# Routed experts: output rows stored by an indirect transfer that leaves out empty slots, and two weight loads that wait for the third expert's slot numbers

## The chip, the cores and the metric

The kernel runs on one core of a Trainium2 chip. The metric is the device time of the program in microseconds; lower is better. The engines are PE (TensorE, matrix products), DVE (VectorE), ACT (ScalarE), POOL (GpSimd) and SP (SyncE, which only issues transfers). Transfers run on 16 DMA engines that all queues share: q1 is SP's queue, q10 ACT's, q0 POOL's.

## The reference

A transformer layer in float32 on 512 tokens of width 1024: a mixer (attention and a state-space branch), cross-attention to 256 memory rows, a mixture of experts, and then a second layer of other form (gated and block-compressed attention and a feed-forward part). The change lies in the mixture of experts:

```python
scores = sigmoid(x2d @ w_router)                 # 512 tokens x 64 experts
# 4 of 8 groups, then 8 experts per token; weights normalised, times 2.5
top_idx = top_k(masked(scores + router_bias), 8)
...
# expert e: its tokens' rows x through two products
out_e = (silu(x @ w_gate[e]) * (x @ w_up[e])) @ w_down[e]   # 1024 -> 256 -> 1024
routed[token] += weight * out_e
y = routed + swiglu(x2d, w_sh_gu, w_sh_down)     # the shared expert
```

512 tokens in 8 experts each are 4096 pairs, 64 per expert on average.

## The kernel before, in words

**Slots.** Each expert has `CAP` = 96 slots. DVE counts, for each chosen expert of a token, the slot that it gets, and from it the row of a table in HBM: row 65 x slot + expert (`PITCH` = 65). An expert's slots fill from 0 up. POOL scatters the tokens' numbers into the table (`slot_table`) by indirect transfers, one round for each of the eight choices k: `scatter_ids(k)`, four transfers each. The table was filled with 512 (`T`) before, so an empty slot reads 512. Experts over 96 tokens have a path of their own, which isn't taken with these inputs. Round k writes the k-th choice of every token in the order of the experts' numbers, so column e of the table is complete after rounds 0 to e for e < 8, and after all eight for the rest.

**Slot numbers.** ACT loads column e of the table into SBUF (`index_column(e)`, after `ids_sent[e]`) for e < 8, and all others in one transfer (`idx_rest`). POOL gathers the rows of x of an expert by an indirect transfer (`gather(e)`) of 96 rows of 4 KB; a slot number over 511 is out of bounds, and no row is read for it.

**The loop over experts.** In `e_block(u, b)` (expert e = 4u + b), PE turns the rows of expert e + 1, multiplies those of e by its gate/up weights (2 MB), and puts in between the down products (1 MB of weights) of expert e - 2. ACT and DVE copy the three parts of an expert's output into `ye[e % 2]` (96 x 1024 f32), and ACT stores all 96 rows into the scratch `y` in HBM with `y_send`: a transfer of 96 rows of 4 KB, 260 KB apart. The copies into the same buffer for expert e + 2 wait until that store has landed (`y_stored`). In the end 32 indirect gathers fetch each token's 8 rows of `y` for the weighted sum.

**Weights.** SP issues them: four gate/up buffers and four down buffers. `refill(e, b)` asks for the gate/up weights of expert e + 4 when `gu_full` says that the product of expert e is done, then for down weights. The first ones are asked for in the order of their buffers' release. Two of them share ring buffers with the shared expert's last panels and are in the list `late`: the gate/up weights of expert 1 and the down weights of expert 0. They are issued when the first gather has landed; the gate/up weights of expert 3 follow them.

**Zeros.** The scratch `y` has a 65th column, which POOL zeroes with 96 rows (`y_pad`).

## Time and profile before

| what | value (us) |
| --- | --- |
| median of 3 runs | 2176.5 (2175.79 to 2177.84) |
| profiled execution, its own time | 2178.47 |
| its span, first to last instruction | 2176.6 |
| PE busy | 2013.4 (93% of the span) |
| DVE, ACT, POOL busy | 773.7, 472.2, 325.5 |
| mean granted PE clock, as a share of full speed | 0.976 |

The span is what the profile shows of the execution. All times of rows below are of this one execution and count from the start of its span. An instruction's row has its start, its duration, its engine and line, what it writes and reads, and in brackets the time its engine stood idle before and what ended that. Rows with q behind the engine's name are transfers being issued; their duration is the issue alone.

### The profile page before, as it was taken

The numbers are of one execution on the slowest core, as the hardware profiler recorded it, in microseconds if no ns is written. First come the engines' busy times: TensorE is split into PE (matmuls) and PEld (weight loads), VectorE is DVE, ScalarE is ACT, GpSimd is POOL, SyncE is SP. The second block draws the span as 40 slices with busy tenths as digits, with TensorE's granted clock in tenths as the row PEclk, the third lists the DMA queues.
The fourth block names the chain that finished last, engine by engine and source line by source line (L and its number), as shares of the span: only waits on it lengthen the run. The fifth ranks groups of instructions, "written<-read, shape, count | busy, mean of one in ns | idle before, by whom it ended". The sixth has DMA issues, their size and how long they took to land.

```text
span 2176.6 us, 25744 instructions
## 1 busy us (share of the span) xinstructions
PE 2013.4 (93%) x10002; PEld 932.7 (43%) x10002; DVE 773.7 (36%) x1606; ACT 472.2 (22%) x1043; POOL 325.5 (15%) x296
## 2 busy tenths in 40 slices
PE   7887999999997999998989999699989899999997
PEld 3334434445543344443334334345655444444443
DVE  5998781214265233332222335501374200000012
ACT  2234431110310333333333332210263000000000
POOL 0653260000025211101010104200032000000000
PEclk9898999999998999999999999899999999999999
DMA  5110014213245999999999977521310222222210
GB/s 227 48 39 1 10 58 163 77 49 126 97 151 180 352 397 400 402 395 390 383 386 384 397 274 254 217 87 68 117 40 1 77 77 77 77 77 77 69 39 29
DMA packets 68579, 368.43 MB, mean 169 GB/s; under 512 B 12194, under 2 KB 12450, under 8 KB 51616
## 3 DMA queue, kind: packets, MB, share of 16 engines
q1 hardware_dynamic: 45216, 300.95, 36.6%
q0 software_dynamic: 12960, 34.13, 4.4%
q10 hardware_dynamic: 10336, 32.45, 4.1%
q8 instruction: 43, 0.70, 0.1%
q14 instruction: 24, 0.20, 0.0%
HBM read 346.35 MB, written 29.92 MB: 173 GB/s over the span
## 4 chain that ended last, share of the span: by engine, by line
PE 69%; DMA 13%; DVE 9%; issue 5%; POOL 2%; ACT 1%; POOLq 0%; SPq 0%; ACTq 0%; DVEq 0%
PE bank L932 41%; PE bank L1263 12%; DMA slab<-w_exp_down 10%; PE bank L1473 6%; PE bank L941 2%; DVE slab L1894 1%; DVE slab L1897 1%; PE bank L1281 1%; DVE work L1891 1%; DVE s5x L1894 1%; POOL slot_table L2619 1%; DVE slab L1891 1%; PE bank L994 1%; DMA slab<-y_rows,yrow_i 1%; DMA slot_table<-tok_i,yrow_i 1%
## 5 line engine op out<-in xcount | busy, mean ns | idle before, releaser
L932 PE MATMUL bank<-slab,ring 128*128 128x512 f32 (+1 forms) x1488 | 632.7, 586 | 12.9 <-DMA ring<-stream 11.2
L932 PEld LDWEIGHTS bank<-slab,ring 128*128 128x128 f32 x1488 | 282.3, 191 | 358.2 <-issue 355.6
L932 PE MATMUL bank<-ring,slab 128*128 128x512 f32 (+1 forms) x608 | 252.6, 576 | 3.8 <-ACT slab L1506 2.0
L1263 PE MATMUL bank<-ring,slab 128*32 128x512 f32 x1536 | 231.7, 605 | 17.7 <-DMA slab<-w_exp_down 14.1
L1263 PE MATMUL bank<-slab 128*32 128x512 f32 x1536 | 227.2, 593 | 22.0 <-DMA ring<-w_exp_down 15.6
L1894 DVE TENSOR_TENSOR slab<-bank,slab 96x256 f32<-96x256 f32 (+3 forms) x120 | 63.8, 532 | 462.6 <-PE bank L932 296.5
L1271 PE MATMUL bank<-ring,slab 128*32 128x512 f32 x512 | 226.1, 594 | 0.0
L2338 DVE COPY slab<-bank 32x512 f32<-32x512 f32 x124 | 80.8, 688 | 407.9 <-PE bank L1271 407.9
L1271 PE MATMUL bank<-slab 128*32 128x512 f32 x480 | 215.0, 601 | 0.0
L932 PEld LDWEIGHTS bank<-ring,slab 128*128 128x128 f32 x608 | 115.6, 191 | 137.4 <-issue 129.4
L2554 POOL TENSOR_TENSOR small<-small 128x1 f32<-128x1 f32 (+2 forms) x30 | 23.0, 765 | 914.6 <-DVE small L1891 913.2
L1473 PE MATMUL bank<-ring,slab 128*128 128x512 f32 x352 | 151.3, 592 | 0.8 <-DVE slab L1894 0.8
L1263 PEld LDWEIGHTS bank<-ring,slab 128*32 128x32 f32 x1536 | 73.1, 111 | 150.7 <-issue 150.4
L2630 POOL DMA_INDIRECT slab<-x_rows,s5x x64 | 61.5, 960 | 507.4 <-PE bank L1225 477.5
L1263 PEld LDWEIGHTS bank<-slab 128*32 128x32 f32 x1536 | 70.5, 110 | 152.2 <-issue 144.3
L1473 PEld LDWEIGHTS bank<-ring,slab 128*128 128x128 f32 x352 | 66.8, 190 | 85.3 <-issue 83.7
L1732 ACT ACTIVATE slab<-bank 32x512 f32<-32x512 f32 x124 | 66.6, 584 | 105.9 <-PE bank L1271 97.4
L1688 ACT ACTIVATE slab<-bank 128x384 f32<-128x384 f32 x128 | 55.8, 488 | 143.5 <-DVE slab L2319 122.0
L1869 ACT ACTIVATE slab<-bank 128x512 f32<-128x512 f32 x22 | 13.1, 597 | 281.8 <-PE bank L932 281.8
L1225 PE MATMUL bank<-const_sb,slab 96*128 96x96 f32 x512 | 53.7, 249 | 13.1 <-DMA slab<-x_rows,s5x 12.2
L941 PE MATMUL bank<-const_sb,work 128*128 128x128 f32 x304 | 48.2, 293 | 18.1 <-DVE work L1891 14.1
L1506 ACT ACTIVATE slab<-bank 128x512 f32<-128x512 f32 (+2 forms) x40 | 22.7, 574 | 181.4 <-PE bank L932 171.6
(275 smaller groups left out, 2144.4 us busy)
## 6 DMA issues: line engine op xcount, KB each, us to landing
ring<-stream SPq DMA_DIRECT2D x171, 512.0 KB, 3.5
slab<-w_exp_gu SPq DMA_DIRECT2D x32, 2048.0 KB
ring<-w_exp_gu SPq DMA_DIRECT2D x32, 2048.0 KB
ring<-w_exp_down SPq DMA_DIRECT2D x32, 1024.0 KB
slab<-w_exp_down SPq DMA_DIRECT2D x32, 1024.0 KB
y_rows<-slab ACTq DMA_DIRECT2D x64, 384.0 KB
gb<-rows ACTq DMA_DIRECT2D x5, 512.0 KB, 5.3
slab<-x_fm SPq DMA_DIRECT2D x1, 2048.0 KB, 9.1
```

What stands on the lines that cost most here:

```text
L932: mm = nc.tensor.matmul(dst, lhs[k], rhs[k], start=(k == 0), stop=(k == len(lhs) - 1))
L941: mm = nc.tensor.transpose(tile(name, i)[0:parts, j * P:(j + 1) * P], x, ident)
L1225: mm = nc.tensor.transpose(bank[j][:, k * CAP:(k + 1) * CAP], xg[b][0:CAP, (4 * j + k) * P:(4 * j + k + 1) * P], ident[0:CAP, 0:CAP])
L1263: mm = nc.tensor.matmul(g_bank[32 * g:32 * g + 32, :], x[:, k, 32 * g:32 * g + 32], w[:, 512 * k:512 * k + 512], start=(k == 0), stop=(k = ...
L1271: mm = nc.tensor.matmul(bank[2 + 3 * t + half][96:128, :], h[:, c * CAP + 32 * t:c * CAP + 32 * t + 32], d[:, c * D + 512 * half:c * D + 5 ...
L1473: return nc.tensor.matmul(tile("fd", 4 * half + t)[:, :], actf[k][:, t * P:(t + 1) * P], panel("fd", 11 * half + k // 2)[:, (k % 2) * 512: ...
L1688: i = nc.scalar.activation(xe[b][:, 4 * j:4 * j + 4, :], bank[j][:, 0:4 * CAP].rearrange("p (k n) -> p k n", n=CAP), ACT.Copy)
L1732: i = nc.scalar.activation(ye[b % 2][0:32, 512 * half:512 * half + 512], bank[2 + half][96:128, :], ACT.Copy)
L1891: return nc.vector.tensor_scalar(out_, in_, s1, s2, op0, op1)
L1894: return nc.vector.tensor_tensor(out_, x, y, op)
L2338: i = nc.vector.tensor_copy(ye[b % 2][32:64, 512 * half:512 * half + 512], bank[5 + half][96:128, :])
L2630: pool.indirect_dma_start(xg[e % 2][0:CAP, :], None, scratch["x2"], bass.IndirectOffsetOnAxis(ap=slot_tok[:, e:e + 1].bitcast(U32), axis=0 ...
```

## The change

Stores: experts 0 to 3 and the last two, 62 and 63, are stored as before, by ACT. The 58 others are stored by POOL with an indirect transfer, `store_rows(e)`, behind the gather of expert e + 6. The list of target rows, `yrow_slot`, is made once by DVE in the block of the sixth expert from the slot numbers: 65 x slot + expert where the slot is filled, and beyond the scratch's bounds where it is empty, so that no row is written. Waits of ACT, DVE and POOL for the stores are split between `y_stored` (direct) and `y_sent` (indirect). The second four experts are written out ahead of the loops of ACT and DVE.

Zeros: since slots are left out, the whole first part of the scratch (96 x 65 = 6240 rows of 4 KB) is zeroed by one transfer that ACT issues before the first attention, in place of POOL's 96 rows.

Weights: the second item of `late` (down weights of expert 0), and with it what SP issues behind it, waits for `idx_landed[2]`, the slot numbers of the third expert.

```diff
@@ sync
-            for x in late:
+            for n, x in enumerate(late):
+                if n == 1:
+                    sp.wait_ge(idx_landed[2], 16)
                 panels_done(*x[:2])
                 x[2]()
@@ scalar
             s5_tables(8)
+            act.dma_start(scratch["y"][0:CAP * PITCH, :], a["zeros"].broadcast_to([CAP * PITCH, D])).then_inc(y_pad, 16)
             for h in range(H1 + 2):
...
-                    y_send(e - 3, (b + 1) % 2)
+                    if send:
+                        y_send(e - 3, (b + 1) % 2)
...
                     if steady:
-                        act.wait_ge(y_stored[b % 2], 16 * (2 * u + b // 2 - 1))
+                        if late:
+                            act.wait_ge(y_sent[b % 2], 16 * (2 * u + b // 2 - 3))
+                        else:
+                            act.wait_ge(y_stored[b % 2], 16 * (2 * u + b // 2 - 1))
...
-            with act.Fori(1, NE // 4 - 1) as u:
+            for b in range(4):
+                e_block(1, b, first=1, send=b < 3, late=False)
+            with act.Fori(2, NE // 4 - 1) as u:
@@ vector
+            for b in range(4):
+                e_block(1, b, first=1, late=False)
+                if b == 1:
+                    for k in range(TOPK):
+                        dve.wait_ge(idx_landed[k], 16)
+                    dve.wait_ge(idx_rest, 16)
+                    link(nc.vector.tensor_copy(slot_f, slot_tok))
+                    link(ts(slot_f, slot_f, T - 0.5, 65536.0, ALU.is_gt, ALU.mult))
+                    tt(yrow_slot, slot_f, row_id, ALU.add).then_inc(y_rows_ready, 1)
@@ gpsimd
-            pool.dma_start(y3[0:CAP, NE, :], a["zeros"].broadcast_to([CAP, D])).then_inc(y_pad, 16)
...
+            def store_rows(e):
+                if e == 4:
+                    pool.wait_ge(y_rows_ready, 1)
+                    pool.wait_ge(y_pad, 16)
+                pool.wait_ge(y0_act, e + 1)
+                pool.wait_ge(y1_dve, e + 1)
+                pool.wait_ge(y2_act, e + 1)
+                pool.wait_ge(y2_dve, e + 1)
+                pool.indirect_dma_start(scratch["y"][0:CAP * PITCH, :], bass.IndirectOffsetOnAxis(ap=yrow_slot[:, e:e + 1].bitcast(U32), axis=0),
+                                        ye[e % 2][0:CAP, :], None, bounds_check=CAP * PITCH - 1, oob_is_err=False).then_inc(y_sent[e % 2], 16)
...
                 gather(e)
+                if e >= 10:
+                    store_rows(e - 6)
+            for e in range(NE - 6, NE - 2):
+                store_rows(e)
```

On POOL, the program before has in the loop nothing but the gathers, one for each expert (the rows from the seventh expert's on; `slab` is the buffer of gathered rows, `x_rows` the rows of x in HBM, `s5x` the slot numbers):

```order
L2630 DMA slab<-x_rows,s5x 96x1024 [waits xtr_full,gathered0,idx_landed6]
L2630 DMA slab<-x_rows,s5x 96x1024 [waits xtr_full,gathered1,idx_landed7]
L2630 DMA slab<-x_rows,s5x 96x1024 [waits xtr_full,gathered0,idx_rest]
L2630 DMA slab<-x_rows,s5x 96x1024 [waits xtr_full,gathered1]
L2630 DMA slab<-x_rows,s5x 96x1024 [waits xtr_full,gathered0]
```

After the change the same place reads as follows (from the ninth expert's gather on; `y_rows` is the scratch y):

```order
L2657 DMA slab<-x_rows,s5x 96x1024 [waits xtr_full,gathered0,idx_rest]
L2657 DMA slab<-x_rows,s5x 96x1024 [waits xtr_full,gathered1]
L2657 DMA slab<-x_rows,s5x 96x1024 [waits xtr_full,gathered0]
L2669 DMA y_rows<-slab,s5x 6240x1024 [waits y1_dve,y2_act,y0_act,y2_dve,y_pad,y_rows_ready]
L2657 DMA slab<-x_rows,s5x 96x1024 [waits xtr_full,gathered1]
L2669 DMA y_rows<-slab,s5x 6240x1024 [waits y2_act,y2_dve,y1_dve,y0_act]
L2657 DMA slab<-x_rows,s5x 96x1024 [waits xtr_full,gathered0]
L2669 DMA y_rows<-slab,s5x 6240x1024 [waits y2_act,y2_dve,y1_dve,y0_act]
```

A store stands now between each two gathers, and a gather is issued only when the store ahead of it has its four waits behind it.

On SP, before, the loads at the end of the shared expert (`w_exp_gu` gate/up, `w_exp_down` down weights) are these:

```order
L817 DMA ring<-w_exp_gu 128x4096 [waits psum_full,gathered0]
L820 DMA ring<-w_exp_down 128x2048 [waits psum_full]
L817 DMA slab<-w_exp_gu 128x4096 [waits psum_full]
L817 DMA ring<-w_exp_gu 128x4096 [waits gu_full] x2
L817 DMA slab<-w_exp_gu 128x4096 [waits gu_full]
```

And after:

```order
L819 DMA ring<-w_exp_gu 128x4096 [waits psum_full,gathered0]
L822 DMA ring<-w_exp_down 128x2048 [waits psum_full,idx_landed2]
L819 DMA slab<-w_exp_gu 128x4096 [waits psum_full]
L819 DMA ring<-w_exp_gu 128x4096 [waits gu_full] x2
L819 DMA slab<-w_exp_gu 128x4096 [waits gu_full]
```

The order of the loads is the same; the second one has a new wait, and all loads behind it stand behind that wait too.

## Rows read from the trace of the kernel before

**Rows 1.** The page, section 1: busy us and share of the span.
```profile
PE 2013.4 (93%) x10002; PEld 932.7 (43%) x10002; DVE 773.7 (36%) x1606; ACT 472.2 (22%) x1043; POOL 325.5 (15%) x296
```

**Rows 2.** Windows of the loop: busy us by engine, granted clock, DMA share, GB/s.
```profile
790.00:965.00 175.00, 169.18 (x1714) 73.61 (x1710) 55.14 (x133) 58.32 (x133) 18.17 (x19) 1.00 1.01 399
965.00:1155.00 190.00, 169.37 (x1718) 71.08 (x1714) 55.12 (x133) 58.33 (x133) 18.18 (x19) 1.00 1.00 386
```

**Rows 3.** Waits of PE, 700 to 1300: total us, times, longest.
```profile
PE bank L1263 <- DMA ring<-w_exp_down: 15.6, 14, 1.8
PE bank L1263 <- DMA slab<-w_exp_down: 14.1, 14, 1.8
```

**Rows 4.** Timeline of SP: gate/up loads at experts 10, 29, 48.
```profile
791.86 0.33 SPq L817 DMA_DIRECT2D slab<-w_exp_gu  x1
967.03 0.33 SPq L817 DMA_DIRECT2D ring<-w_exp_gu  x1
1157.03 0.33 SPq L817 DMA_DIRECT2D ring<-w_exp_gu  x1
```

**Rows 5.** DMA queues in 965 to 1155: packets, MB, share of 16 engines.
```profile
q1 hardware_dynamic: 5527, 60.53, 82.0%
q10 hardware_dynamic: 2121, 7.44, 10.6%
q0 software_dynamic: 2118, 5.36, 7.5%
```

**Rows 6.** Queue q0 in 899.9:901, in 899.9:907, and in 983.5:984.6.
```profile
q0 software_dynamic: 22, 0.03, 8.8%
q0 software_dynamic: 112, 0.17, 6.5%
q0 software_dynamic: 20, 0.08, 19.1%
```

**Rows 7.** Timeline before the loop and in its start: us, duration, engine, [idle before].
```profile
672.11 0.33 SPq L817 DMA_DIRECT2D ring<-w_exp_gu  x1
673.82 0.72 SPq L817 DMA_DIRECT2D slab<-w_exp_gu  x1
674.68 0.99 POOL L2630 DMA_INDIRECT slab<-x_rows,s5x  x1 [0.30 <-issue]
683.98 1.54 PE L1225 MATMUL bank<-const_sb,slab 96*128 96x96 f32 x8 [8.85 <-DMA slab<-x_rows,s5x]
690.42 0.99 POOL L2630 DMA_INDIRECT slab<-x_rows,s5x  x1 [7.83 <-DMA s5x<-slot_table]
703.60 0.38 PE L1232 MATMUL bank<-const_sb,slab 96*128 96x96 f32 x2 [1.14 <-issue]
```

**Rows 8.** Window after the loop's start.
```profile
684.00:706.00 22.00, 19.92 (x126) 7.17 (x130) 6.33 (x14) 2.57 (x7) 10.04 (x11) 0.87 0.55 200
```

**Rows 9.** Timeline of POOL and ACT in the loop, and queue q0 in 909:915.2.
```profile
905.03 0.96 POOL L2630 DMA_INDIRECT slab<-x_rows,s5x  x1 [8.35 <-PE bank L1225]
...
905.77 0.32 ACTq L1712 DMA_DIRECT2D y_rows<-slab  x1
917.37 1.08 ACT L1732 ACTIVATE slab<-bank 32x512 f32<-32x512 f32 x2 [1.05 <-PE bank L1271]
920.72 0.38 ACT L1694 ACTIVATE slab<-bank 96x256 f32<-96x256 f32 x1 [2.28 <-PE bank L1263]
...
q0 software_dynamic: 110, 0.30, 12.7%
```

**Rows 10.** ACT at 157, that window, SP's first issues (min/median/max ns), q1 in 0:13.
```profile
157.43 1.28 ACT L1526 ACT_TABLE_LOAD   x1
...
157.00:225.00 68.00, 54.09 (x214) 29.52 (x212) 58.65 (x101) 30.33 (x74) 24.17 (x18) 0.87 0.01 2
...
L805 SPq DMA_DIRECT2D ring<-stream x12: 421/647/2285, 1.2 to 12.4; - x12
...
q1 hardware_dynamic: 589, 3.75, 77.3%
```

More of the change, by code:

```diff
@@ L650, in build @@
         ovn, ovincl, none64 = rt(64), rt(64), rt(64)
+        row_id, slot_f = rt(64)[0:CAP, :], rt(64)[0:CAP, :]
         wsum, wk = rt(4), sm(32)
@@ L658, in build @@
         slot_tok = s5x[0:CAP, 3072:3072 + NE].bitcast(I32)
+        yrow_slot = s5x[0:CAP, 3136:3200].bitcast(I32)
         no_token = s5x[0:120, 3072:3072 + NROW // 120].bitcast(I32)
@@ L750, in build @@
         gu_landed, dn_landed = [sem(f"gu_landed{j}") for j in range(4)], [sem(f"dn_landed{j}") for j in range(4)]
-        y_stored = [sem("y_stored0"), sem("y_stored1")]
+        y_stored, y_sent = [sem("y_stored0"), sem("y_stored1")], [sem("y_sent0"), sem("y_sent1")]
         xtr_full, xe_ready, gu_full, silu_ready = sem("xtr_full"), sem("xe_ready"), sem("gu_full"), sem("silu_ready")
@@ L759, in build @@
         diag_ready, pe_combined = sem("diag_ready"), sem("pe_combined")
-        combined, y_zeroed, y_pad = sem("combined"), sem("y_zeroed"), sem("y_pad")
+        combined, y_zeroed, y_pad, y_rows_ready = sem("combined"), sem("y_zeroed"), sem("y_pad"), sem("y_rows_ready")
         act_ready = sem("act_ready")
@@ L898, in _ @@
             for b in range(2):
-                sp.wait_ge(y_stored[b], 16 * NE // 2)
+                sp.wait_ge(y_stored[b], 48)
+                sp.wait_ge(y_sent[b], 16 * (NE // 2 - 3))
         @block.tensor
@@ L1707, in y_send @@
             def y_send(e, b):
+                if e == 0:
+                    act.wait_ge(y_pad, 16)
                 act.wait_ge(y2_act, e + 1)
@@ L1711, in y_send, with e_block @@
                 act.wait_ge(y2_dve, e + 1)
-                act.dma_start(y3[0:CAP, bass.ds(e, 1), :].rearrange("r e d -> r (e d)"), ye[b][0:CAP, :]).then_inc(y_stored[b], 16)
-            def e_block(u, b, first=0, last=NE):
+                act.dma_start(y3[0:CAP, e, :], ye[b][0:CAP, :]).then_inc(y_stored[b], 16)
+            def e_block(u, b, first=0, last=NE, send=False, late=True):
                 e = 4 * u + b
@@ L1750, in _ @@
             y_rest(NE - 3, 1)
-            y_send(NE - 3, 1)
             for b in range(2):
-                act.wait_ge(y_stored[b], 16 * (NE // 2 - 1))
+                act.wait_ge(y_sent[b], 16 * (NE // 2 - 3))
                 y_full(b, 5 - 5 * b, dnf_full, b + 1, yf_act)
@@ L1759, in _ @@
             for b in range(2):
-                act.wait_ge(y_stored[b], 16 * NE // 2)
+                act.wait_ge(y_stored[b], 48)
+                act.wait_ge(y_sent[b], 16 * (NE // 2 - 3))
             n_ov = act.value_load(ctrl_i[0:1, NOV:NOV + 1], min_val=0, max_val=NOV)
@@ L2319, in y_rest, with e_block @@
                 nc.vector.tensor_copy(ye[b][64:96, 768:1024], bank[4][96:128, 0:256]).then_inc(y2_dve, 1)
-            def e_block(u, b, first=0):
+            def e_block(u, b, first=0, late=True):
                 e = 4 * u + b
@@ L2335, in e_block @@
                     if steady:
-                        dve.wait_ge(y_stored[b % 2], 16 * (2 * u + b // 2 - 1))
+                        if late:
+                            dve.wait_ge(y_sent[b % 2], 16 * (2 * u + b // 2 - 3))
+                        else:
+                            dve.wait_ge(y_stored[b % 2], 16 * (2 * u + b // 2 - 1))
                     for half in range(2):
@@ L2342, in _ @@
                 e_block(0, b)
-            with dve.Fori(1, NE // 4) as u:
+            for b in range(4):
[7 more added lines that the diff above has]
+                    tt(yrow_slot, slot_f, row_id, ALU.add).then_inc(y_rows_ready, 1)
+            with dve.Fori(2, NE // 4) as u:
                 for b in range(4):
@@ L2350, in _ @@
             for b in range(2):
-                dve.wait_ge(y_stored[b], 16 * (NE // 2 - 1))
+                dve.wait_ge(y_sent[b], 16 * (NE // 2 - 3))
                 y_full(b, 5 - 5 * b, dnf_full, b + 1, yf_dve)
@@ L2355, in _ @@
             for b in range(2):
-                dve.wait_ge(y_stored[b], 16 * NE // 2)
+                dve.wait_ge(y_stored[b], 48)
+                dve.wait_ge(y_sent[b], 16 * (NE // 2 - 3))
             n_ov = dve.value_load(ctrl_i[0:1, NOV:NOV + 1], min_val=0, max_val=NOV)
@@ L2603, in _ @@
             nc.gpsimd.memset(none64, 0.0)
+            nc.gpsimd.iota(row_id, [[1, NE]], base=0, channel_multiplier=PITCH, allow_small_or_imprecise_dtypes=True)
             nc.gpsimd.memset(chosen[:, 256:320], 0.0)
@@ L2639, in _ @@
                 gather(e)
+                if e >= 10:
+                    store_rows(e - 6)
+            for e in range(NE - 6, NE - 2):
+                store_rows(e)
             pool.wait_ge(route_ctrl, 3)
             pool.wait_ge(xtr_full, NE)
-            pool.wait_ge(y_pad, 16)
             for b in range(2):
-                pool.wait_ge(y_stored[b], 16 * NE // 2)
+                pool.wait_ge(y_stored[b], 48)
+                pool.wait_ge(y_sent[b], 16 * (NE // 2 - 3))
             n_ov = pool.value_load(ctrl_i[0:1, NOV:NOV + 1], min_val=0, max_val=NOV)
```

2 lines of the change are left out of this document (1 added, 1 removed).

## The prediction

> **What bounds the kernel now.** The page first: TensorE (PE) is busy for 93% of the span [rows 1]. From 700 to 1300 us runs the loop over the 64 routed experts, and the windows show that the DMA engines are full there too, so I read it by stretches. From 790 to 965 us PE is busy for 169.2 of 175 us, from 965 to 1155 for 169.4 of 190, at the same granted clock of 1.00 and a DMA share of 1.01 and 1.00 [rows 2]. What ended PE's idle time in the loop was above all the down weights, 15.6 + 14.1 = 29.7 us [rows 3]. When it happened is read from SyncE (SP): it asks for a new gate/up matrix each time an expert's gate/up product is done, so its L817 rows are a clock of the experts. 19 experts from 791.86 to 967.03 take 9.22 us each; 19 from there to 1157.03 take 10.0 each [rows 4]. So the weights were ahead of PE at first, lost 0.8 us of their lead with each expert, and set the pace from about the 29th expert on. Less DMA work pays only there, or earlier by keeping the lead.
>
> **The bytes.** In 965 to 1155 the weights (q1) take 82.0% of the engines' time, the y stores (q10) 10.6%, the gathers (q0) 7.5% [rows 5]. The gathers carry 5.36 MB for 19 experts, 69 rows of 4 KB each out of 96; a y store always carries 96. The change makes 58 stores (experts 4 to 61) indirect and leaves empty slots out. 512 tokens in 8 experts each fill 4096 slots, 64 an expert, so it removes 58 x 32 = 1856 rows, 7.6 MB, and at the 386 GB/s of that stretch [rows 2] 19.7 us of DMA time. That would be the gain if every byte less brought the weights earlier.
>
> I doubt it, for a reason that the trace gives. A weight matrix is usable when all 16 engines have delivered their share, so the fullest engine counts, not the mean. How are the rows of an indirect transfer dealt out? A gather makes 112 packets: 96 rows, of which the empty ones are under 512 B, and 16 for the semaphore. The one read from 899.9 us moved 0.17 MB, 41 full rows; in its first 1.1 us it made 22 packets with 0.03 MB, about 7 full and 15 empty [rows 6]. Were the rows dealt in turn, each engine would have two or three full ones at its head, and 22 packets on 16 engines would nearly all be full. In a fuller expert's gather they are: 20 packets, 0.08 MB [rows 6]. So some engines have full rows only and others empty ones only: neighbouring slots, six by six, lie on one engine, and as an expert's slots fill from 0, the empty ones always fall to the last engines. The work per expert is then, for a full engine, 8.20 (weights, 0.820 x 10.0) + 1.06 (store) + 0.75 x 96/69 = 1.04 (gather) = 10.3 us, beside a measured period of 10.0 (packets overlap a little), and for the last engine 8.20 + 1.06 = 9.3. The change takes the empty store rows from the last engines only: 10.3 stays 10.3, and 9.3 becomes 8.2. By this the 7.6 MB are worth nothing, but that full engines share the memory with less traffic. The trace has no price for that; it lies between 0 and 0.34 us an expert (0.131 MB at 386 GB/s). I take 0.05, near the lower end, because it is a side effect of 3% of the traffic, over the 36 experts from the 29th on: 2 us.
>
> The Trainium skill ("DMA: Bandwidth & Descriptors", section "The descriptor swizzle") says that each engine of a transfer writes a fixed set of neighbouring partitions. By that rule, too, the empty rows lie on the same few engines, and the packets here agree; dealt evenly, the sum would be 19.7 us instead of 2.
>
> **The held weights.** After the shared experts PE stands still for 8.85 us, until at 683.98 the rows of the second expert have landed; their gather was issued at 674.68 [rows 7]. Just before, SP had issued 2 + 1 + 2 MB of weights, the first at 672.11 and the last at 673.82 [rows 7]. In the same load the third expert's slot numbers were on their way: GpSimd (POOL) waited 7.83 us for them, until 690.42 [rows 7]. The change lets only the 2 MB at 672.11 go; the down weights of the first expert and the gate/up weights of the fourth, behind them on SP, wait for the third slot numbers. 2.1 MB at 386 GB/s are 5.4 us, so the engines are free near 679 and the gather should land near 681 (gain 3), the slot numbers near 682. The held 3 MB run from there to 690, when the engines were used at 0.55 before (684 to 706 [rows 8]), and are first needed by the third and fourth experts, after 700. Behind the wait on SP stand the refills; the first needs the first expert's product, which starts after 684 anyway. The third gather comes some 7 us earlier, and the 1.14 us that PE waits at 703.6 [rows 7] can go. Bounds: 0 (the chain of ids and slot numbers waits elsewhere) and 5; I take 4. It counts although the weights set the end, since each refill follows PE's product and the engines are not yet full there [rows 8].
>
> **Added work, at nothing.** POOL issues a store behind each gather, another 0.96 us in a period in which it idles 8.35 [rows 9]. The store leaves at 906.3 instead of 905.77 and stands behind the gather on one queue; now the gather's last packets run until 915 [rows 9], so I put the store's end near 917. ACT's next copy into that buffer starts at 917.37, and 2.28 us are free behind it [rows 9]: a store up to 2 us later is hidden, and beyond that it delays each expert. DVE waits for the same stores, later in the period. Its three small operations on slot numbers stand in an engine busy for 55.1 of 190 us [rows 2]. The zeros, 6240 rows or 25.6 MB, are issued by ScalarE (ACT) at about 157.4, are 66 us of DMA work at 386 GB/s, and find engines that move 2 GB/s [rows 10]; nothing needs them before 700. Nothing, then, as long as ACT is free after its issue.
>
> Sum: 4 + 2 = 6 us. The profiled run took 2178.5 (span 2176.6) and the median is 2176.5; from the median the forecast is **2170.5 us**.
>
> **Rivals.**
> *The bytes count in full* (0.22). For it: the DMA share of 1.00 [rows 2]; with the last engines idle for 10% of the time it should be about 0.97. Then 19.7 us of DMA work go, PE has 29.7 us of such waits to give, and with the 4 at the start the time is 2153.
> *ACT is held by the zeros* (0.22; slower). At the start SP issued 16 transfers of 8 rows an engine in a row, and the issues grew to 2.29 us, from a least of 0.42 [rows 10]: with much in flight, an issue waits. Of those 144 packets an engine (8 rows and a semaphore each) 589/16 = 37 were through at 13 us [rows 10], so about 107 could be outstanding. The zeros are 390 an engine. If the limit is near 107, some 283 must drain first: 283/390 of 66 us = 48 us in which ACT computes no softmax, in a stretch in which it is busy for 30.3 of 68 us and PE waits on its chain [rows 10]. Price 48 less 6: 2218.5. It decides as soon as ACT is held for over 6 us. 
> *No net change* (0.20). The store lands 2 to 3 us late, ACT's copy slips and the experts from the 8th to the 61st pay 0.1 us each, 5 us, against the 6: 2175.5, within -4 to +4.
> *The forecast* (0.36), own range 2166 to 2174.
>
> **How the numbers follow.** 0.2%, 4.4 us, is about what a measurement of this kernel can tell from no change. Of the forecast's 0.36, 0.27 lie beyond it; with the 0.22 of the full bytes and 0.03 of no net change, faster is 0.52. Within it lie 0.09 + 0.13 = 0.22, slower are 0.22 + 0.04 = 0.26. The range must reach into both outer cases: 2151 below; above, the held case lies anywhere from some us to 48, and 2212 leaves about half of it out.
>
> **What would show it.** Right: the L817 rows again 10 us apart in the middle of the loop, PE waiting for down weights; PE's wait before the first expert near 6 us instead of 8.85; ACT's issue of the zeros under 1 us. Full bytes: periods of 9.2 to 9.5 throughout. Held: an issue of tens of us at 157, and PE behind ACT until 210. Late store: ACT waiting for y_rows in every period. The forecast is wrong above all if the issue holds ACT, or if a store's rows are dealt to the engines otherwise than a gather's.

## The result, and the profile after

The changed kernel took 2199.98 us (2198.62 to 2202.68, 4 runs), the kernel before 2177.1 on the same chip: a ratio of 1.0107 (95% interval 1.009 to 1.0125), 22.9 us slower. The forecast of 2170.5 has the wrong sign; the range held the value only because it reached out to a rival that did not happen.

The page of the profiled run after the change, against [rows 1] and [rows 3] (busy time and idle time before; then queues):

```profile
span 2196.8 us, 25741 instructions
PE 2020.9 (92%) x10002; PEld 933.0 (42%) x10002; DVE 773.8 (35%) x1609; ACT 472.9 (22%) x1043; POOL 382.4 (17%) x354
...
L1268 PE MATMUL bank<-ring,slab 128*32 128x512 f32 x1536 | 232.8, 607 | 30.2 <-DMA slab<-w_exp_down 27.0
L1268 PE MATMUL bank<-slab 128*32 128x512 f32 x1536 | 231.6, 601 | 30.4 <-DMA ring<-w_exp_down 22.2
```

PE waits 27.0 + 22.2 = 49.2 us for down weights, where it waited 29.7. The stretches of [rows 2], now:

```profile
790.00:965.00 175.00, 161.07 (x1631) 68.89 (x1624) 52.28 (x126) 56.23 (x128) 34.61 (x36) 1.00 0.99 366
965.00:1155.00 190.00, 163.39 (x1658) 68.81 (x1650) 54.41 (x132) 57.02 (x131) 34.61 (x36) 1.00 0.98 359
```

SyncE's gate/up issues are again the clock of the experts; these answer to [rows 4]:

```profile
791.97 0.33 SPq L819 DMA_DIRECT2D slab<-w_exp_gu  x1
...
865.73 0.33 SPq L819 DMA_DIRECT2D slab<-w_exp_gu  x1
875.28 0.33 SPq L819 DMA_DIRECT2D slab<-w_exp_gu  x1
885.68 0.33 SPq L819 DMA_DIRECT2D ring<-w_exp_gu  x1
...
1194.11 0.33 SPq L819 DMA_DIRECT2D slab<-w_exp_gu  x1
1206.38 0.33 SPq L819 DMA_DIRECT2D slab<-w_exp_gu  x1
...
1286.62 0.33 SPq L819 DMA_DIRECT2D slab<-w_exp_gu  x1
```

At 792 us the two kernels are level (791.86 before). The change costs nothing up to there, and everything behind it: the last of these issues is at 1286.62, before it was at 1265.78, 20.8 us of a span that is 20.2 longer. PE sets the pace only until 865.73, where it did until 967.03 [rows 4], eleven experts more; then 30 experts take (1194.11 - 885.68) / 30 = 10.28 us each, and the last nine, (1286.62 - 1194.11) / 9, as much; before, the last 30 take (1265.78 - 967.03) / 30 = 9.96. Fewer bytes are to be moved, and they move more slowly: 366 and 359 GB/s in place of the 386 of [rows 2] and more.

Where in an expert's period is the rate lost? The windows can be laid by the gather's issue on GpSimd. Its packets start some 4 us after it. For two gathers each, the 3 us that begin 1 us after the issue, and the 3 us that begin 5 us after it, before the change (issues at 1039.67 and 1049.74; the last column is GB/s, the one ahead of it the DMA engines' busy share):

```profile
1040.70:1043.70 3.00, 3.00 (x32) 1.10 (x28) 0.00 (x0) 0.89 (x3) 0.00 (x0) 1.00 1.04 423
1044.70:1047.70 3.00, 3.00 (x40) 1.26 (x32) 0.52 (x1) 0.44 (x2) 0.00 (x0) 1.00 1.03 388
1050.70:1053.70 3.00, 3.00 (x32) 0.92 (x28) 0.00 (x0) 1.17 (x3) 0.00 (x1) 1.00 0.99 404
1054.70:1057.70 3.00, 3.00 (x39) 1.14 (x31) 0.78 (x2) 0.39 (x2) 0.00 (x0) 1.00 1.02 391
```

And after it (issues at 1041.33 and 1051.83):

```profile
1042.30:1045.30 3.00, 3.00 (x32) 1.10 (x28) 0.00 (x0) 0.00 (x0) 0.95 (x2) 1.00 0.99 425
1046.30:1049.30 3.00, 3.00 (x36) 1.25 (x32) 0.00 (x0) 0.72 (x3) 0.00 (x0) 1.00 0.95 280
1052.80:1055.80 3.00, 3.00 (x32) 1.09 (x31) 0.00 (x0) 0.00 (x0) 0.95 (x2) 1.00 0.99 425
1056.80:1059.80 3.00, 3.00 (x36) 1.15 (x32) 0.00 (x0) 0.64 (x2) 0.00 (x0) 1.00 0.99 296
```

The engines are busy for 0.95 and 0.99 of the time there, but while the gather's rows move they carry 280 and 296 GB/s where they carried 388 and 391. The queues of the second stretch, before:

```profile
DMA packets 206, 1.16 MB, mean 388 GB/s; under 512 B 36, under 2 KB 36, under 8 KB 138
q1 hardware_dynamic: 73, 0.75, 65.1%
q10 hardware_dynamic: 64, 0.25, 22.8%
q0 software_dynamic: 69, 0.17, 15.0%
```

and after:

```profile
DMA packets 168, 0.84 MB, mean 280 GB/s; under 512 B 51, under 2 KB 51, under 8 KB 94
q1 hardware_dynamic: 82, 0.66, 74.8%
q0 software_dynamic: 86, 0.18, 20.6%
```

Before, 0.75 + 0.17 = 0.92 MB were read in 3 us, 307 GB/s, and 0.25 MB of y rows written beside them. After, 0.84 MB are moved in all, 280 GB/s, and no queue but the weights' and GpSimd's has a share in it: the store stands behind the gather in GpSimd's queue, and its rows go later, when reads alone would reach 425. The experiments ask what part of the change makes this.

### The profile page after: what moved, and what is told of

Its sections match the earlier page's. It is cut to its first block, busy times and chain, and to the rows that moved or that the text cites. A ratio compares the mean times of both kernels' runs of the same rounds, so it can differ in the third digit from the quotient of the medians.

```text
span 2196.8 us, 25741 instructions
## 1 busy us (share of the span) xinstructions
PE 2020.9 (92%) x10002; PEld 933.0 (42%) x10002; DVE 773.8 (35%) x1609; ACT 472.9 (22%) x1043; POOL 382.4 (17%) x354
## 4 chain that ended last, share of the span: by engine, by line
PE 67%; DMA 18%; DVE 9%; issue 4%; POOL 1%; ACT 1%; SPq 0%; POOLq 0%; DVEq 0%; ACTq 0%
PE bank L937 42%; DMA slab<-w_exp_down 16%; PE bank L1268 10%; PE bank L1478 6%; PE bank L946 2%; DVE slab L1908 1%; DVE slab L1911 1%; DVE work L1905 1%; PE bank L1286 1%; DVE s5x L1908 1%; PE bank L999 1%; DVE slab L1905 1%; PE bank L1340 1%; PE bank L1076 1%; PE bank L1382 1%
## 5 line engine op out<-in xcount | busy, mean ns | idle before, releaser
L1268 PE MATMUL bank<-slab 128*32 128x512 f32 x1536 | 231.6, 601 | 30.4 <-DMA ring<-w_exp_down 22.2
L2669 POOL DMA_INDIRECT y_rows<-slab,s5x x58 | 54.9, 947 | 60.2 <-issue 34.5
## 6 DMA issues: line engine op xcount, KB each, us to landing
y_rows<-zeros ACTq DMA_DIRECT2D x1, 24960.0 KB, 126.9
```

The lines of the kernel that those rows point to most:

```text
L1268: mm = nc.tensor.matmul(g_bank[32 * g:32 * g + 32, :], x[:, k, 32 * g:32 * g + 32], w[:, 512 * k:512 * k + 512], start=(k == 0), stop=(k = ...
L2669: pool.indirect_dma_start(scratch["y"][0:CAP * PITCH, :], bass.IndirectOffsetOnAxis(ap=yrow_slot[:, e:e + 1].bitcast(U32), axis=0), ye[e % ...
```

## The experiments

In all of them the kernel before ran on the same chip; a ratio is to it. A diff is against the changed kernel or against "the hold alone" (the first one), as said.

**1. The hold alone.** The kernel before, with this on SyncE:

```diff
-            for x in late:
+            for n, x in enumerate(late):
+                if n == 1:
+                    sp.wait_ge(idx_landed[2], 16)
```

> The kernel before with one line of the change: the gate/up load of expert 1 and the down load of expert 0 wait for the third expert's slot numbers; the stores are as before. In the changed kernel the gate/up issue of expert 8 stood at 764.4 us against 773.3 before. Theory 1 (the hold alone removes the 13 us stall of the first gather, and the store takes the time back later): this run starts the expert phase 9 us earlier, is PE-paced at 9.2 us an expert until expert 22 or so, then goes at 10.0 us an expert by its DMA, and ends between 2170 and 2177 us, since what the weights start earlier only the DMA bound can keep. Rival (the start gain comes from the missing full-width stores): the stall stays and the time is 2175 to 2178 us.

2172.73 us against 2180.43, a ratio of 0.9969 (0.9954 to 0.9984): 0.3% faster. Its last gate/up issue is at 1261.66, 4.1 us ahead of the kernel before, of which 1.6 are there by 790.27. The 9 us that I expected at the start came from pairing issues of different experts (the two kernels are level at 792, as shown above). The hold is a small gain, and the loss lies in the rest of the change, the stores above all.

**2. All rows written by index.** The changed kernel with

```diff
-link(ts(slot_f, slot_f, T - 0.5, 65536.0, ALU.is_gt, ALU.mult))
+link(ts(slot_f, slot_f, T - 0.5, 0.0, ALU.is_gt, ALU.mult))
```

> The changed kernel with the store's offset for empty slots multiplied by 0 in place of 65536: the same indirect stores from GpSimd's queue, but all 96 rows are written. Theory 1 (what slows the DMA engines is the way by which rows go, the software queue with rows by index, not their number): the weight-bound period rises above 10.3 us an expert, the added 7.6 MB cost up to 20 us, 2205 to 2220 us. Theory 2 (leaving rows out unbalances the engines, and the even load of before would bring the 386 to 400 GB/s back): about 2177 us.

2195.68 us, 1.007 (1.0055 to 1.0086), in the range of neither theory. PE waits 26.5 + 24.8 us for down weights, and the middle of the loop reads

```profile
965.00:1155.00 190.00, 162.63 (x1650) 68.51 (x1646) 55.18 (x133) 57.16 (x131) 35.57 (x37) 1.00 1.00 372
```

Writing 32 rows more per expert costs nothing beside the changed kernel (1.0107 and, below, 1.0086), and an even load does not bring the rate back: by SyncE's issues at 884.64 and 1192.41, 30 experts take 10.26 us each, where the changed kernel's take 10.28. The engines are now busy for 1.00 of the time and carry 372 GB/s, with the empty rows left out 0.98 and 359. That fits rows left out on engines that then stand idle; no trace here tells the engines apart.

**3. No row written.** The same line with `-0.5` in place of `T - 0.5`, so that all slots count as empty and the 58 experts' rows of the output are missing.

> The changed kernel with 65536 added to the offset of every slot, so that the 58 indirect stores are issued but write no row at all (the output lacks these experts' rows): what stays is their issue and their empty descriptors. Theory 1 (rows that move by index are what costs, in the time of their own packets and in that of the packets beside them): the rate of the weights' packets returns to that of before or better, a period of 9.2 to 9.5 us an expert throughout, 2145 to 2160 us. Rival (issue and descriptors cost, whatever they carry): the period stays at 10.2 to 10.3 us and the time near 2195 us.

2162.9 us, 0.9921 (0.9905 to 0.9937). The time is near the first forecast, but its reason is not borne out: the low rate beside the gather is still there. The stretch 1 us behind the gather at 1041.11, and those 5 us behind it and behind the one at 1050.54:

```profile
1042.10:1045.10 3.00, 3.00 (x33) 0.91 (x29) 0.00 (x0) 0.53 (x2) 0.95 (x1) 1.00 1.03 429
1046.10:1049.10 3.00, 3.00 (x41) 1.23 (x30) 1.00 (x2) 0.62 (x2) 0.00 (x0) 1.00 0.93 302
1055.50:1058.50 3.00, 3.00 (x40) 1.38 (x33) 1.02 (x2) 0.54 (x2) 0.00 (x0) 1.00 0.97 311
```

So 58 stores of 96 rows, done away with altogether, are worth only 10 us beside the hold alone (2172.73, same chip). The time alone would hide a larger gain, since PE's own pace is a floor (2155.5 us in experiment 9), but it was not reached: from 1019.44 to the last issue at 1254.14, 24 experts take 9.78 us each, where the hold alone takes 9.87 (from 965.69 to 1261.66, 30 experts). 0.39 MB less an expert, 1.0 us at 386 GB/s, is worth 0.1 us there, and PE's pace lasts six experts longer: much of the stores' work had cost next to nothing.

**4. The same place and queue, without an index.** The changed kernel with

```diff
-pool.indirect_dma_start(scratch["y"][0:CAP * PITCH, :], bass.IndirectOffsetOnAxis(ap=yrow_slot[:, e:e + 1]...), ye[e % 2][0:CAP, :], ...)
+pool.dma_start(y3[0:CAP, e, :], ye[e % 2][0:CAP, :]).then_inc(y_sent[e % 2], 16)
```

> The changed kernel with the 58 stores as plain transfers of all 96 rows, issued from GpSimd's queue at the same place behind the gather. Theory 1a (the software queue itself slows the engines): like all_rows, 2205 to 2220 us. Theory 1b (only rows by index do): period 10.0 us as before, 2170 to 2178 us.

2193.08 us, 1.0061 (1.0044 to 1.0079), 20.4 us over the hold alone on the same chip and, like experiment 2, in the range of neither theory. The index is not it: a plain transfer in that place does the same (300 GB/s in the stretch beside the gather at 1039.51):

```profile
1040.50:1043.50 3.00, 3.00 (x32) 1.10 (x28) 0.00 (x0) 0.00 (x0) 0.54 (x1) 1.00 1.00 429
1044.50:1047.50 3.00, 3.00 (x40) 1.25 (x35) 0.12 (x1) 0.72 (x2) 0.00 (x0) 1.00 1.00 300
```

After these four my theory was that two transfers standing in the software queue slow every packet. The next four were made to tell that.

**5. Both.** Experiment 3's empty stores from GpSimd, and beside them all 64 stores of 96 rows from ScalarE as before (`if send:` made `if True:`, and both semaphores waited for).

> The hold and the stores of 96 rows from ScalarE's queue as before, and besides GpSimd's 58 indirect stores with every offset out of bounds: a second transfer in the software queue that moves no row. The kernel with such empty stores alone moved 3.0 to 3.6 MB less weight-bound time but only 355 to 361 GB/s against 386 to 398. Theory 1 (a second transfer standing in GpSimd's queue slows every packet of the engines for some 4 us of each expert, whatever it carries): the same bytes as before at 355 to 370 GB/s, a period of 10.5 to 10.8 us in the weight-bound part, 2195 to 2225 us. Rival (the low rate of the empty stores was only that less was asked for): 2170 to 2177 us as with the hold alone.

2174.86 us, 0.9988 (0.9969 to 1.0006). The theory falls: two transfers of GpSimd's queue for each expert, and the rate beside the gather at 1045.06 is that of the kernel before.

```profile
1050.10:1053.10 3.00, 3.00 (x40) 1.26 (x32) 0.48 (x1) 0.48 (x2) 0.00 (x0) 1.00 1.00 389
```

Beside 3 it says more: the one thing added is written bytes, 4 x 96 KB an expert, and the engines carry some 80 GB/s more in that stretch, as if these bytes cost nothing there. Over the whole run they do cost something: experiment 5 is by the ratios 0.67%, 15 us, above 3. And since 5 has everything of the tested change but the move itself (the zeros, the list of target rows, GpSimd's second transfer), it says what the rest of the change costs beside the hold alone: 0.9988 against 0.9969, about 4 us and within the noise.

**6. Empty stores of 16 slots.** Experiment 3 with `[0:16]` in place of `[0:CAP]` on both sides.

> The changed kernel with empty indirect stores of 16 slots in place of 96 (no row is written for 58 experts). Theory 1a (the price of the second transfer is per descriptor): a sixth of the price is left, 380 GB/s and more in the loop until PE sets the pace, 9.2 us an expert nearly throughout, about 2140 to 2155 us. Theory 1b (the price is that of a second transfer in the queue, however short): 355 to 361 GB/s as with 96 empty slots, 2160 to 2165 us.

2163.95 us, 0.9947 (0.993 to 0.9963); from 790 to 900 us 361 GB/s, as with 96 empty slots. I had taken that low rate for the price of the second transfer as such. But PE is busy there for 106.25 of 110 us, its own pace, so 361 is all that is asked for; after 5 the run says that no price of the empty store can be measured at either length.

**7. The two apart.** The changed kernel, the store at the gather's old place and the gather behind the next y copy:

```diff
                     pool.wait_ge(xtr_full, e - 1)
+                if e >= 10:
+                    store_rows(e - 6)
+                    pool.wait_ge(y0_act, e - 4)
                 pool.indirect_dma_start(xg[e % 2][0:CAP, :], None, scratch["x2"],
...
-                if e >= 10:
-                    store_rows(e - 6)
```

> The changed kernel with its two software transfers of an expert apart: the store is issued first, at the place where the gather was, and the gather some 4 us later, behind the next expert's y copy on ScalarE; each has its 4 us before its packets begin, so that they no longer stand in the queue together. Theory 1 (two in the queue at once are what slows the packets): the packets return to the rate beside one gather, 386 GB/s and more, with 0.25 MB less an expert than before, a period of 9.2 to 9.6 us, 2150 to 2170 us. Rival (each software transfer costs its own, wherever it stands): two such stretches in an expert in place of one, period 10.3 us, 2190 to 2205 us.

2222.23 us, 1.0209 (1.0169 to 1.0248). The worst of all, against 2150 to 2170 expected, and above the rival's 2190 to 2205 too.

**8. The hold alone, with a late gather.** Experiment 1 with `pool.wait_ge(y0_act, e - 4)` ahead of the gather from expert 10 on; the stores go from ScalarE as before.

> The hold, the stores as before, and the gather some 4 us later in the expert, so that it no longer stands beside ScalarE's store. Its tiles have 10 us to spare. If one software transfer beside a store of the hardware queue costs something as well, the weight-bound period falls below 10.0 us, 2160 to 2170 us; if not, 2170 to 2176 us as with the hold alone.

2217.99 us, 1.0187 (1.0144 to 1.0231), 47 us over experiment 1 by the two ratios, although nothing is added; both expected ranges were missed. From 790 to 1300 us PE waits for gathered rows for 0.5 us in all, so the late gathers are in time; it waits 54.3 us for down weights. The gathers at 1044.62 and 1054.82 have lost the store beside them: 310 (second line) and 303 GB/s. The store, issued at 1038.36, goes ahead of the gather, beside weights alone (first line):

```profile
1043.40:1046.40 3.00, 3.00 (x40) 1.25 (x35) 0.23 (x1) 0.62 (x2) 0.96 (x1) 1.00 1.03 434
1049.60:1052.60 3.00, 3.00 (x36) 1.09 (x32) 0.00 (x0) 0.87 (x2) 0.00 (x0) 1.00 1.02 310
```

434 GB/s is hardly more than the 423 that the weights reach by themselves in the kernel before: in these 3 us 1.00 MB of weights and 0.30 MB of y rows moved, where there it was 1.27 MB of weights. Beside weights alone the store's bytes take the place of weights. Beside the gather they don't: 0.77 MB of weights in the second line without the store, 0.75 in the kernel before with it. This made the second theory: **while a gather's rows are read, all reads together move at about 300 GB/s; a store then goes beside them for nothing.** Experiment 8 is the hold alone with one thing changed, which transfer lies beside which, and it loses about twice what the tested change loses. The theory doesn't give that size: by it the two should lose about the same. That is open.

**9. Hardly any gather.** The hold alone, with `bounds_check=0` for `T - 1` in the gather, so that only token 0's row is read.

> The hold, the stores of 96 rows from ScalarE's queue as before, and a gather whose bounds let only token 0 through, so that next to no row of x is read (the experts' inputs are stale). The last four kernels felled the theory of two transfers in one queue: empty stores beside the stores as before cost nothing (386 to 400 GB/s), and the gather moved away from the store cost 45 us. Theory 2: while the gather's rows are read, some 4 us of each expert, what is read moves at no more than about 300 GB/s, and the store's written bytes go beside it for nothing; a store put behind the gather in its queue loses that place. Then without the gather the rate stays above 400 GB/s throughout, PE sets the pace, 9.2 us an expert, and the time is 2140 to 2150 us. Rival (the store beside the gather matters for another reason, and the gather costs only its bytes, 0.26 MB an expert or 0.7 us): period 9.3 to 9.6 us, 2150 to 2160 us.

2155.51 us, 0.9904 (0.9879 to 0.9929). By the time alone that is the rival's (2150 to 2160). PE is busy for 290.11 of the 300 us from 900 to 1200, which is the share of the PE-paced stretch of [rows 2], at 384 GB/s, all that it then asks for. The period can't decide between the two: the gather's bytes alone, 0.7 us of 10.0, would leave 9.3, and PE's pace is 9.2.

```profile
900.00:1200.00 300.00, 290.11 (x2929) 125.73 (x2925) 92.88 (x224) 100.02 (x228) 30.70 (x32) 1.00 1.00 384
```

The stretches decide. With the weights and the store in flight, 5 us after the gather's issue at 1046.0, the engines move 432 GB/s, and 422 after the one at 1055.25:

```profile
1051.00:1054.00 3.00, 3.00 (x39) 1.51 (x32) 1.24 (x2) 0.75 (x2) 0.00 (x0) 1.00 1.09 432
```

So neither the weights nor the store are slow in that stretch by themselves. Against the hold alone the gathers cost about 0.65%, 14 us; the loop then goes at PE's own pace and cannot go faster, and my 2140 to 2150 was 5 us too low.

**10. Stores of 64 rows.** The hold alone, ScalarE's stores of slots 0 to 63 only, and the changed kernel's zeros on ScalarE. Rows of fuller experts are lost.

> The hold, the fill with zeros of the changed kernel, and plain stores from ScalarE's queue of the first 64 slots alone (rows of experts with more tokens are lost). Theory 2 (written bytes beside the gather are free): a third fewer written bytes are worth next to nothing, 2168 to 2174 us. Rival (bytes count in full, 7.6 MB at 386 GB/s are 20 us): 2150 to 2158 us.

2171.3 us, 0.9971 (0.9956 to 0.9986), the same as the hold alone. A third of the stores' bytes is worth nothing that can be measured in the time, and neither do 25.6 MB of zeros cost anything there. The two could cancel, but not by much: PE is busy for as long beside the zeros as without them (last section), and in the one execution traced the loop from the tenth expert on, 792.49 to 1259.64, is 4.2 us shorter than in the hold alone, where that one and the kernel before, with the same loads and stores there, differ by 2.5.

**11. Store first.** Experiment 7 without `pool.wait_ge(y0_act, e - 4)`: the store directly ahead of the gather.

> The changed kernel with the two software transfers swapped and nothing between them: the store's rows are first in each engine's queue and the gather's behind them. Theory 2: neither order puts them beside each other, the period stays near 10.3 us, 2190 to 2205 us. Rival (the order decides, since the store is then as early as ScalarE's was): about 2172 us.

2216.74 us, 1.0186 (1.0154 to 1.0217): slower than the changed kernel, which I had not expected. An early store is no help by itself; in the kernels that keep the rate it goes beside the gather, from another queue. Why this order is worse than the other by 0.9 to 1.0% is open. Single waits of PE reach 3.5 us in it, where they were at most 1.8, and the mean granted clock from 965 to 1155 is 0.96; that this makes the difference is not shown.

**12. The changed kernel again.**

> The changed kernel once more, so that its time stands beside the others of this chip: 2198 to 2203 us, 1.0 to 1.2% over the kernel before. The kernel that writes all 96 rows by index took 1.0070 of before, the changed one 1.0107 on another chip; if leaving rows out costs something by itself this one stays over 1.009, if it was the chip it falls to 1.007.

2196.07 us, 1.0086 (1.006 to 1.0112). The interval overlaps that of experiment 2 (1.0055 to 1.0086) and that of the first measurement, the time lies below the 2198 to 2203 expected, and the ratio between the two that I had named. Leaving rows out gains nothing. Whether it costs a few us is open: the first measurement by itself (1.009 to 1.0125) lies above experiments 2 and 4, this one does not.

What holds the reads at 300 GB/s? Three more kernels were made for this question.

**13. Plain rows.** The hold alone, and for the gather a plain transfer of x's rows 0 to 63 (wrong inputs for the experts):

```diff
-pool.indirect_dma_start(xg[e % 2][0:CAP, :], None, scratch["x2"], ...)
+pool.dma_start(xg[e % 2][0:64, :], scratch["x2"][0:64, :]).then_inc(gathered[e % 2], 16)
```

> The hold, the stores as before, and in place of the gather by index a plain transfer of rows 0 to 63 of x from the same queue: about the bytes of the gather, but the rows are consecutive and no index is used (the experts' inputs are wrong). Without the gather's rows the kernel went at PE's pace throughout, 9.2 us an expert, 0.96% under the kernel before. If it is the index or the scatter of the rows that holds reads at 300 GB/s, this one ends near it, 2150 to 2160 us; if reading 64 rows of x in any order does it, it stays near the kernel with the hold alone, 2168 to 2176 us.

2163.96 us, 0.9936 (0.992 to 0.9951), between the two cases. The dip is there without an index: 374 and 380 GB/s with the store beside it, of which 0.93 MB in 3 us, 310 GB/s, are read in the first (gathers at 1041.1 and 1050.39). So the index does not make it:

```profile
1042.10:1045.10 3.00, 3.00 (x32) 1.10 (x28) 0.00 (x0) 1.25 (x3) 0.00 (x0) 1.00 0.99 414
1046.10:1049.10 3.00, 3.00 (x39) 1.38 (x32) 0.87 (x2) 0.48 (x2) 0.00 (x0) 1.00 1.06 374
```

But this transfer costs half of what the gather costs. By the prediction's reckoning its 64 rows lie four to each of 16 engines, instead of six on the fullest. That fits, but no trace here tells the engines apart, so it is argued, not shown.

**14. Rows from elsewhere.** The hold alone, the gather by the same indices from the first 2 MB of the gate/up weights (wrong inputs).

> The hold, the stores as before, and the gather by the same indices, but its rows read from the first 2 MB of the experts' gate/up weights (the experts' inputs are wrong). If the rate falls because of where x's rows lie in memory, this one loses the fall and ends at 2150 to 2160 us; if because rows are read by index, 2168 to 2176 us as with the hold alone.

2172.26 us, 0.9965 (0.995 to 0.998), as with the hold alone. Behind the gather at 1046.06, with the store beside it, 0.92 MB in 3 us are read, 307 GB/s as before the change:

```profile
1051.10:1054.10 3.00, 3.00 (x38) 1.09 (x31) 0.74 (x2) 0.38 (x1) 0.00 (x0) 1.00 0.99 399
```

**15. Rows spread.** The hold alone, x's rows nine rows apart (`"x2_rows", (T * XS, D)`, token numbers times `XS = 9`), the region filled with zeros first; what the kernel computes stays the same.

> The hold, the stores as before, and x's rows nine rows apart in memory (18.9 MB in place of 2.1, filled with zeros from ScalarE's queue while the DMA is idle), gathered by index; the output is the reference's. If the rows' nearness in 2 MB is what holds reads at 300 GB/s while they are gathered, the rate rises to 410 GB/s there and the time is 2150 to 2162 us, the fastest version; if not, 2168 to 2176 us.

2170.19 us, 0.9961 (0.9947 to 0.9974), not distinguishable from the hold alone (0.9969). Behind the gather at 1046.46 the engines move 408 GB/s in the same stretch, of which 313 are read. With 14 it says that the place of the rows does not matter to what can be measured here.

## Why the prediction was wrong

**What bounds the kernel now: right.** Experiment 9 gives PE's pace to the end as soon as the DMA work shrinks enough, and every kernel here moves with the weights' rate in the loop.

**The bytes: right in size.** Forecast: 2 us of a possible 19.7. Measured: nothing, by two ways, 10 against 1 (0.9971 and 0.9969) and 12 against 2. The reason given, that the empty rows fall to engines that have time, fits where the stores are GpSimd's: a period of 10.28 us with 0.13 MB less against 10.26 with all rows, at a busy share of 0.98 in place of 1.00. The Trainium skill ("DMA: Bandwidth & Descriptors", section "The descriptor swizzle") gives each engine of a transfer to 128 partitions a set of partitions of its own, in two groups of four neighbours; the share of 0.98 agrees with such a split, but no run here counts rows by engine. Where the stores lie beside the gather there is a second reason, which I did not see: they cost next to nothing anyway (experiments 3 and 10). So the right size owes something to luck.

**The held weights: the first steps right, the gain given back, the total near.** The rows of the second expert were forecast for 681, and PE's wait ahead of the first product for 6 us. PE in the changed kernel, against [rows 7]:

```profile
681.48 1.54 PE L1230 MATMUL bank<-const_sb,slab 96*128 96x96 f32 x8 [6.40 <-DMA slab<-x_rows,s5x]
...
695.21 0.88 PE L1230 MATMUL bank<-const_sb,slab 96*128 96x96 f32 x8 [3.65 <-DMA slab<-x_rows,s5x]
```

The third gather was also 7 us earlier as forecast, at 683.59. But SyncE let the held loads go at 682.81 and 683.19, as soon as the slot numbers were there:

```profile
682.81 0.33 SPq L822 DMA_DIRECT2D ring<-w_exp_down  x1
683.19 0.42 SPq L819 DMA_DIRECT2D slab<-w_exp_gu  x1
```

They ran ahead of the third gather, whose rows landed at 695.2, and PE waited 3.65 us for them. I had the held 3 MB in engines that are half idle and did not ask what stands behind them. Alone the hold gave 0.31% (0.16 to 0.46), 7 us against the 4 forecast; its profiled execution was 3.0 us shorter. That the total came near is partly luck: only 1.6 us were there at 790 us, and no row shows where the rest of the 7 comes from.

**"Added work, at nothing": the step that failed.** The prediction put the store "behind the gather on one queue", reckoned its end to 917 and asked only whether ScalarE would wait for it. On that question it was nearly right. In the stretch at PE's pace (790 to 870 us) ScalarE's y copy does wait for the late store in every period, up to 4.7 us, but most of that it would have waited for PE; from 838 to 866 us 0.83 to 1.75 of the 2.28 us free behind it are left, so the copy slips by at most 1.5, and the experts stay 9.22 us apart. In the middle of the loop (965 to 1155) it waits for PE alone:

```profile
ACT slab L1744 <- DMA y_rows<-slab,s5x: 40.1, 9, 4.7
...
ACT slab L1744 <- PE bank L1276: 77.0, 18, 4.5
ACT slab L1700 <- PE bank L1268: 44.3, 19, 2.4
```

What was mis-sized is the move itself: 0 in the sum, 20.4 us measured (experiment 4 against 1, same chip), for a plain store just as for one by index. Experiment 4 has the rest of the change in it too; against experiment 5, which has that rest without the move, it is 0.73%, 16 us. So the move cost 16 to 20 us. The hold's 7 and these 20 make the +13 us of experiment 4; the changed kernel was 17 and 23 us slower than the kernel before, and what makes the 4 to 10 us beyond that (the 4 are within the noise) is open. The reckoning "8.20 + 1.06 + 1.04" took a packet's time to be the same wherever it stands, so that moving a store by a few us inside a full period could cost nothing. It could have been read from the trace of before: [rows 9] has the store issued 0.7 us behind each gather, thus beside it, and the windows of the kernel before, shown above, have 388 GB/s of which 0.25 MB in 3 us are writes, while the same engines 4 us earlier carry 404 to 423, all of it weights. The loss has two parts by SyncE's issues: PE's pace ends eleven experts earlier, 11 x 1.06 = 11.7 us, and the period behind it is 10.28 us in place of 9.96, 30 x 0.32 = 9.6 us; together 21.3 of the 20.8 found. What in the chip slows the reads beside the gather stays open.

**The rivals.** Bytes in full fell in experiment 10, which has the zeros and the small stores and gains nothing. ScalarE held by the zeros fell in the profile:

```profile
156.29 0.64 ACTq L1581 DMA_DIRECT2D y_rows<-zeros  x1
```

0.64 us for 390 rows an engine, where I priced 48. The Trainium skill ("Perfetto Trace Analysis", section "DMA Instruction — HWDGE (DVE, Sync)") has the issuing sequencer free only when all descriptors are generated. No row here shows when they were; what the row shows is that neither that nor a full buffer held ScalarE: it was free after 0.64 us, 126 us before the last row landed. Late store: its sign, ScalarE waiting for y rows in every period, is there up to 870 us, but costs nothing by the rows above. No rival was slower by the mechanism that made the kernel slower. That the range held the measured value is luck: its upper part was there for the zeros.

## What to carry to other kernels

Before a transfer is moved to another queue or a few microseconds along, look at which transfers lie beside it now, and at the rate and the kinds of traffic in that stretch; a period in which the DMA engines are busy for 1.00 can hold work that costs next to nothing, and the move makes it cost. Here that was writes beside the gather's reads of 4 KB rows, and one late issue of the gather cost about twice what the whole change did. A saving in bytes counts only in a stretch where those bytes are the limit; try it alone before building the machinery for it.

## What the runs showed of the hardware

- While the gather's rows of 4 KB were on their way and no store lay beside them, the engines moved 280 to 311 GB/s (changed kernel, experiments 3, 4 and 8), and 418 to 429 in the first three of these 4 us earlier, busy in both. With a store beside, 388 to 391 GB/s (before, experiment 5). What was read, weights and gathered rows together, was 300 to 313 GB/s with the store and without it (before, experiments 3, 5, 8 and 13 to 15) and no more than 280 and 296 in the changed kernel: rows by index or in order, from x, from x spread over 18.9 MB or from the weights. With a store but no gather the two together reached 422 and 432, 320 of the latter read (experiment 9). What in the chip limits the reads is open; shorter or longer rows were not tried, nor was dealing the filled slots to all 16 engines.
- The zeros, a transfer from DRAM to DRAM whose source is one row read again and again, used the engines for 0.99 of the time and moved half of what the loop moves. From 157 to 257 us:

```profile
DMA packets 5078, 20.78 MB, mean 208 GB/s; under 512 B 16, under 2 KB 16, under 8 KB 5072
q10 hardware_dynamic: 5031, 20.61, 99.4%
```

They took 126.9 us where the prediction had 66, with no effect: PE is busy for 125.5 us between 157 and 300 us in both kernels.
- After a wait of under 2 us PE can run at a lower granted clock, and that cost nothing here. At the end of the changed loop the experts from 1194.11, 1224.88 and 1255.78 took 12.3, 12.4 and 12.3 us. The first of them in stretches of 2 us (the third column from the right is the granted clock):

```profile
1196.00:1198.00 2.00, 0.61 (x8) 0.34 (x12) 1.04 (x3) 0.61 (x2) 0.98 (x1) 1.00 1.05 442
1198.00:1200.00 2.00, 2.00 (x15) 0.54 (x8) 0.00 (x0) 0.00 (x0) 0.95 (x1) 0.52 0.98 418
1200.00:1202.00 2.00, 2.00 (x16) 0.70 (x12) 0.00 (x0) 0.00 (x0) 0.00 (x0) 0.62 0.99 352
1202.00:1204.00 2.00, 2.00 (x24) 0.78 (x20) 0.00 (x0) 1.07 (x2) 0.00 (x0) 1.00 1.02 289
```

PE waits 1.68 us for down weights, until 1197.39, and then runs for some 4 us at 0.52 and 0.62 of the full 2.4 GHz, near the lower level of 1.2 GHz, with 15 and 16 matmuls in 2 us and 24 in the next 2. The kernel before has one such expert in the loop, of 12.4 us from 1157.03, behind a wait of 1.82 us. In the middle of the changed loop waits of up to 1.7 us left the clock at 1.00, so that such a wait may or may not cost it. The lower clock is no part of the loss: the two experts behind each slow one took 9.05 to 9.45 us, and all nine from 1194.11 on 10.28 us each like the thirty ahead of them, so the weights set the pace there. In experiments 7, 8 and 11, with longer waits, the mean clock from 965 to 1155 is 0.96 to 0.97; whether that is a part of their loss is not shown.
- An indirect store whose offsets are all out of bounds costs nothing in the kernel's time that could be measured beside plain ones (0.9988 in experiment 5, 0.9969 for the hold alone, with overlapping intervals); its issue keeps GpSimd busy for 0.95 us.
